# Key products behind each query block, 11 of 16 lists searched before the dense tiles: one change to a fused decoder layer on one core

## Chip, cores and metric

One core of a Trainium2 chip runs the whole layer in one launch. The metric is the device time of the program in microseconds (us); lower is better. Engines are written as in the profile: PE is the matrix engine, DVE the vector engine, ACT the scalar engine, POOL the GpSimd engine, SP the queue that issues most loads.

## What is computed

A decoder layer over 512 tokens of width 1024: a mixer (short convolution and a gated recurrence), cross-attention into 256 memory tokens, and a retrieval layer (PEER). The change lies almost wholly in the retrieval layer:

```
q = (tokens @ w_query).reshape(Ntok, 8, 2, 128)            # 8 heads, 2 halves: 16 queries of 128
s = einsum('nhpd,hpkd->nhpk', q, sub_keys)                  # 16 lists of 128 scores per token
s_top, i_top = top_k(s, 16)                                 # the 16 best of each list
cand = s_top[:, :, 0, :, None] + s_top[:, :, 1, None, :]    # per head: sums of a pair of lists
best, pos = top_k(cand, 16); gate = softmax(best)           # 16 experts per head
y = sum over h, e of gate_e * gelu(expert_down[e] . x) * expert_up[e]
```

There are 16384 experts (128 blocks of 128).

## The kernel before, in words

Tokens stand in four tiles of 128. Tiles 0 to 2 are "dense": for them the kernel multiplies all 16384 down rows with the tokens (128 **down blocks**, each 24 matrix products over 352 token columns), builds a gate matrix with zeros where an expert isn't chosen, and multiplies with all up rows. Tile 3 (`ST`) is "sparse": its 128 chosen rows per token are gathered from memory by POOL (indirect DMAs) and DVE takes the dot products. The last 32 tokens of dense tile 2 (the "edge") are treated in the same way, with 32 further gathers. So there are 160 gathers and 160 dots in all.

Every weight block is loaded by SP into a ring of 5, rounded by ACT (`high`, L577), and the rest is computed by POOL (`low`, L457). PE waits for `low_ready` of a block, ACT's `high(p)` waits until PE is done with block p-3, and `ahead(b)` is `high(b+2)`. In the retrieval layer the order of work is written out by hand on each engine:

- **Query blocks.** PE computes 16 of them (`columns(68 + n, ...)`), the first eight over 512 tokens and the others over 384. They give list 8 to 15 first and then 0 to 7 (for the sparse tile, lists 0 to 7 come from raw weights before). ACT copies each out (L780, L782).
- **Key products.** PE multiplies queries with keys, 128 by 128 each, in float32. For the sparse tile four groups of four (L1707) are done, two ahead of the query blocks, two behind query block 8. For the dense tiles, 12 groups of four (L1733) follow behind the last query block, each copied out by ACT (L802).
- **Choice.** DVE (`top16`) searches lists: `max` (L1177), `max_index` and `match_replace` (L1181, L1182), `max` (L1186), `max_index` (L1190). `choose` then makes candidates (L1204 to L1210), searches those, writes L1217 (`best_ready`), and turns positions into indices (L1221 to L1246). It is done for the sparse tile first, whose end (L1265, `idx_ready`) lets POOL gather. Then come the dense tiles in the order 2, 0, 1 (`CHOSEN`). Tile 2 ends with L1288 (`idx_ready` 2), the others with gate pieces (L1277 to L1280, `hk_ready` 1 and 2). Between the searches DVE does dots (L1170): 12 in the score lists of a tile, 4 in the candidates, 6 in the rest, 66 in all (`DOTS_A`).
- **Down blocks before the gates.** Meanwhile PE does `AHEAD` = 60 down blocks. PE's `first_product(i)` also waits for the `gelu` of block i-2. ACT's `early_at(i)` is `high` for block i+2, then `gelu` of block i (L814), then a store (L816). Behind `EXP_AT` = 16, 32, 52 blocks ACT waits for `best_ready` of a tile and takes an exponential (L840); behind two more blocks of the first group it waits for `idx_ready` 2 and moves edge indices (L848). Ahead of block 40 and of block 59 PE waits for `hk_ready` 1 and 2 and transposes (L1776).
- **Gate steps.** 48 of them follow, each beside a down block (L1748), with about 1.7 gathers and dots each, and then the remaining 20 down blocks with 14 gathers (`DOTS_END`). Then come the up blocks, 128 of 18 products.

POOL's loop at that place is `low(84 + i)`, then gathers `down_row(k)`: 5 at i = 0, 2 at i = 1, and from there about 1.13 per block, in a ring of 7 slots. Gather k waits until the dot of k-7 is done.

Of the kernel before, what the change touches and what calls it, by code (L numbers as in the profile page):

```python
# [13 lines left out]
P = 128  # L14
# [14 lines left out]
NK = 128  # L29
# [13 lines left out]
CHOSEN = (DT - 1,) + tuple(range(DT - 1))  # L43
EXP_AT = (16, 32, 52)
TURN_AT = (20, 40, 60)
AHEAD = TURN_AT[-1]
# [20 lines left out]
ROWS = SLOTS + EDGE_SLOTS  # L67
FIRST_EDGE = 44
GEL_AT, SPLIT_AT, LAST_TURN = 12, 20, 28
DOTS_SCORES = (3, 3, 3, 3)  # L70
DOTS_CAND = (1, 1, 1, 1)
DOTS_HOT = 6
DOTS_A = DT * (sum(DOTS_SCORES) + sum(DOTS_CAND) + DOTS_HOT)
DOTS_STEP = (0, 0) + (2,) * 10 + (1, 2, 2) * 12
DOTS_END = (1,) * 14
ROWS1, COLS2 = 3, 4
CANDS = ROWS1 * TK + (TK - ROWS1) * COLS2
UPPER = 0xFFFF0000
FIRST_GATHER = 0
KEEP = 16  # L80
# [23 lines left out]
def build(nc, x_in, mem_in, vecs_in, final_in, ffn_in, front_w, keys_in, down_in, down_rows, up_in, out, gate_dram, hid_dram):  # L104
    ctx = ExitStack()
    with ctx:
# [104 lines left out]
        dense_k, sparse_k = TopK(108, 124, 5), TopK(184, 92, 2)  # L211
        hk = dense_k.hk
        esum = at(27.75, 16)
        hkT = at(132.5, 5 * DN // 2).bitcast(BF16).rearrange("p (a n r) -> p a n r", a=5, r=2)
# [61 lines left out]
        QB = (6, 7, 0, 1)  # L276
        SB = (0, 1, 2, 0)
        KEY_ORDER = (2, 3, 0, 1)
        PB = (0, 2, 4, 5, 0, 2, 4, 5, 0, 2, 0, 2)
        bank_free = sem("bank_free")  # L280
# [13 lines left out]
        qp_out, pk_done, pk_out = sem("qp_out"), sem("pk_done"), sem("pk_out")  # L294
        KS = 4
        qs_out = sem("qs_out")
# [136 lines left out]
        def _(pool):  # L433
# [57 lines left out]
            for i in range(AHEAD + 2):  # L491
                low(FRONT + i)
                if i == FIRST_GATHER:
                    pool.wait_ge(idx_ready, 1)
                    while k < 5:
                        down_row(k)
                        k += 1
                if i == FIRST_GATHER + 1:
                    while k < RING_A:
                        if k == 5:  # L500
                            pool.wait_ge(pk_done, KS + 4 * DT)
                        down_row(k)
                        k += 1
                while k < DOTS_A and i > FIRST_GATHER and (k - RING_A) * (AHEAD - 8 - FIRST_GATHER) < (i - FIRST_GATHER - 1) * (DOTS_A - RING_A):
                    down_row(k)
                    k += 1
# [30 lines left out]
        def _(act):  # L537
# [49 lines left out]
            def ahead(b):  # L587

                high(b + 2)
# [72 lines left out]

            def keys_out(block, b):
                ahead(block)
                act.wait_ge(block_used, block + 1)
                nc.scalar.activation(KT[:, b, :], psum[:, b % 2, 0:NM], ACT.Copy).then_inc(k_out, 1)
# [13 lines left out]
            nc.scalar.activation(junk[:, SEQ:2 * SEQ], junk[:, 0:SEQ], ACT.Exp, scale=-0.5).then_inc(conv_root, 1)  # L680
            keys_out(31, 3)
            for b in range(32, 36):
                ahead(b)
                act.wait_ge(conv_y, CC + b - 31)
                nc.scalar.activation(hT_half[0][:, b - 32, :], pB[:, b - 32, :], ACT.Copy).then_inc(y_high, 1)
            values_out(0, 2)
            for b in range(4, 8):
                keys_out(32 + b, b)
            def kv_high_part(n):
# [94 lines left out]

            sparse_query_out(0)
            norm_high(ffnn)
            high(QPOS)
            sparse_query_out(1)
            high(QPOS + 1)
            sparse_key_out(0)  # L790
            sparse_key_out(1)
            for n in range(16):
                query_out(n)
                if n == 8:
                    sparse_key_out(2)
                    sparse_key_out(3)
            for c in range(4 * DT):
                if c == 8:
                    high(USED + 2)
                act.wait_ge(pk_done, KS + c + 1)  # L800
                g = KEY_ORDER[c // DT]
                nc.scalar.activation(score[:, c % DT, g * 512:(g + 1) * 512], psum[:, PB[c], :], ACT.Copy)\  # L802
                    .then_inc(pk_out, 1)
                if c == 3:
                    act.wait_ge(best_ready, 1)
                    nc.scalar.activation(sparse_k.ebest, sparse_k.ebest, ACT.Exp).then_inc(e_ready, 1)
            def early_at(i):
# [13 lines left out]

            for i in range(4):
                early_at(i)
# [126 lines left out]
        def _(dve):  # L950
# [243 lines left out]

            def choose(scores, u, k, between_scores, between_cand, between_hot, hk, hk_free, copied=(None,)):

                for part, groups in enumerate(copied):
                    if groups is not None:
                        dve.wait_ge(pk_out, groups)
                    each = 16 // len(copied)  # L1200
                    k = top16([(scores[:, j * NK:(j + 1) * NK], u.top[:, j, :], u.topi[:, j, :].bitcast(U32))
                               for j in range(part * each, (part + 1) * each)], k, between_scores)
                pairs = u.pairs.bitcast(BF16).rearrange("p (a r) -> p a r", r=2)
# [48 lines left out]
            def gates_of(u, dst, exps):  # L1252
# [10 lines left out]
            step(nc.vector.tensor_copy(psum[:, 3, 0:P], at(205.5, P)))  # L1263
            choose(score[:, ST, :], sparse_k, 0, (0, 0, 0, 0), (0, 0, 0, 0), 0, sparse_k.hk, 0, (2, KS))
# [8 lines left out]
            dve.wait_ge(pk_out, KS + 4 * DT)  # L1273
            kd = 0
# [7 lines left out]
            for n, t in enumerate(CHOSEN):  # L1282
                kd = choose(score[:, t, :], dense_k, kd, DOTS_SCORES, DOTS_CAND, DOTS_HOT, hk if n else hk_last, max(n - 1, 0))
                if n:
# [140 lines left out]
        def _(pe):  # L1425
# [289 lines left out]
            pe.wait_ge(ffnn.ready, KC)  # L1715
            pe.wait_ge(ffns.high, 2)
            for n in range(16):
                if n >= 4:
                    pe.wait_ge(qp_out, n - 3)
                columns(68 + n, hT_half, SEQ if n < 16 - RAW else DN, 4 + n % 4)  # L1720
                if n == 8:
                    pe.wait_ge(qp_out, 8)
                    sparse_keys(2)
                    pe.wait_ge(pk_out, 1)
                    sparse_keys(3)
            pe.wait_ge(pk_out, KS)
            for c in range(4 * DT):
                g, t = KEY_ORDER[c // DT], c % DT
                pe.wait_ge(qp_out, max(c // DT * 4 + 4, {4: 13, 5: 14}.get(PB[c], 0)))
                if c >= 4:  # L1730
                    pe.wait_ge(pk_out, KS + (c - 1 if c >= 10 else c - 3))
                for hp in range(4 * g, 4 * g + 4):
                    ins = nc.tensor.matmul(psum[:, PB[c], hp % 4 * NK:(hp % 4 + 1) * NK], qpT[:, hp, t * P:(t + 1) * P],  # L1733
                                           keysT[:, hp, :], start=True, stop=True)
                ins.then_inc(pk_done, 1)

# [30 lines left out]

            pe.wait_ge(pk_out, KS + 8)
            def turn_indices(n, indices, split):
# [8 lines left out]

            for i in range(AHEAD):
                if i == TURN_AT[1]:  # L1780
                    turn_indices(1, hk, hk[:, 2:5, :])
# [78 lines left out]
```

## Time and profile before

| | us |
|---|---|
| median of 3 runs (lowest, highest) | 1619.19 (1617.63, 1620.11) |
| the profiled execution's own time | 1619.37 |
| its span, first to last instruction | 1617.6 |
| PE busy in the span | 1597.2 |
| DVE, ACT, POOL busy | 1140.9, 665.7, 820.0 |

The 1.8 us between the span and the time of the execution lie around the program. A row of the timeline reads: start, duration, engine and line, operation, what it wrote and read, how many such instructions in a row, and in brackets how long the engine had been idle before and who released it.

### The profile page before, as it was taken

The numbers are of one execution on the slowest core, as the hardware profiler recorded it, in microseconds if no ns is written. First come the engines' busy times: TensorE is split into PE (matmuls) and PEld (weight loads), VectorE is DVE, ScalarE is ACT, GpSimd is POOL, SyncE is SP. The second block draws the span as 40 slices with busy tenths as digits, with TensorE's granted clock in tenths as the row PEclk, the third lists the DMA queues.
The fourth block names the chain that finished last, engine by engine and source line by source line (L and its number), as shares of the span: only waits on it lengthen the run. The fifth ranks groups of instructions, "written<-read, shape, count | busy, mean of one in ns | idle before, by whom it ended". The sixth has DMA issues, their size and how long they took to land.

```text
span 1617.6 us, 25384 instructions
## 1 busy us (share of the span) xinstructions
PE 1597.2 (99%) x9227; PEld 1423.1 (88%) x9227; DVE 1140.9 (71%) x2214; ACT 665.7 (41%) x995; POOL 820.0 (51%) x523
## 2 busy tenths in 40 slices
PE   8999999999999999999999999999999999999998
PEld 6888888888889999999999999998888888888886
DVE  4155451351509999997999997339888888888887
ACT  5352442441534344434444544443333333333333
POOL 4463276423244989996877777856222222222220
PEclk9999999999999999999999999999999999999999
DMA  5332243313434999997999999949999999999992
GB/s 196 92 103 71 76 150 96 104 53 118 151 97 136 348 338 337 333 349 236 330 407 400 400 412 402 357 145 398 396 337 348 333 350 334 350 335 347 340 330 77
DMA packets 154442, 424.96 MB, mean 263 GB/s; under 512 B 15728, under 2 KB 65904, under 8 KB 154224
## 3 DMA queue, kind: packets, MB, share of 16 engines
q1 hardware_dynamic: 89088, 229.41, 41.5%
q0 software_dynamic: 41472, 151.01, 25.2%
q10 hardware_dynamic: 23792, 43.33, 7.0%
q8 instruction: 58, 0.95, 0.2%
q14 instruction: 32, 0.26, 0.0%
HBM read 379.88 MB, written 43.25 MB: 262 GB/s over the span
## 4 chain that ended last, share of the span: by engine, by line
PE 90%; DVE 4%; ACT 2%; POOL 2%; DMA 1%; issue 1%; DVEq 0%; SPq 0%; ACTq 0%
PE psum L1459 28%; PE psum L1461 27%; PE psum L1460 27%; PE psum L1748 4%; POOL w_low L457 1%; DMA hid_dram<-arena 1%; PE psum L1695 1%; ACT kept L547 1%; POOL arena L486 1%; DVE arena L1069 0%; ACT w_high L577 0%; PE psum L1582 0%; DMA kept<-x_in 0%; DVE hT_low L1041 0%; PE psum L1431 0%
## 5 line engine op out<-in xcount | busy, mean ns | idle before, releaser
L457 POOL TENSOR_TENSOR w_low<-kept,w_high 128x1024 fp32r<-128x1024 f32 x212 | 520.1, 2457 | 309.3 <-ACT w_high L577 307.5
L1459 PE MATMUL psum<-hT_high,w_high 128*128 128x352 f32 (+2 forms) x1408 | 483.9, 344 | 6.2 <-POOL w_low L457 6.1
L1461 PE MATMUL psum<-hT_high,w_low 128*128 128x352 f32 (+2 forms) x1408 | 477.1, 339 | 0.0
L1460 PE MATMUL psum<-hT_low,w_high 128*128 128x352 f32 (+2 forms) x1408 | 476.5, 338 | 0.0
L1459 PE MATMUL psum<-up_high,wgt_high 128*128 128x512 f32 x768 | 299.0, 389 | 0.0
L1460 PE MATMUL psum<-up_low,wgt_high 128*128 128x512 f32 x768 | 299.0, 389 | 0.0
L1461 PE MATMUL psum<-up_high,wgt_low 128*128 128x512 f32 x768 | 299.0, 389 | 0.0
L1459 PEld LDWEIGHTS psum<-hT_high,w_high 128*128 128x128 f32 x1408 | 265.3, 188 | 21.6 <-ACT arena L814 3.7
L577 ACT ACTIVATE w_high<-kept 128x1024 fp32r<-128x1024 f32 x212 | 223.7, 1056 | 128.1 <-PE psum L1461 91.2
L1460 PEld LDWEIGHTS psum<-hT_low,w_high 128*128 128x128 f32 x1408 | 265.1, 188 | 12.4 <-issue 0.5
L1461 PEld LDWEIGHTS psum<-hT_high,w_low 128*128 128x128 f32 x1408 | 264.8, 188 | 12.6
L581 ACT ACTIVATE up_high<-arena 128x1024 fp32r<-128x1024 f32 x128 | 135.8, 1061 | 314.3 <-PE psum L1461 310.1
L1170 DVE CUSTOM_DVE_ANT_0 arena<-arena,psum 128x1024 f32<-128x1024 f32 x160 | 190.4, 1214 | 37.0 <-DMA arena<-down_rows,kept 36.4
L1341 DVE TENSOR_TENSOR up_low<-arena,up_high 128x1024 fp32r<-128x1024 f32 x128 | 156.8, 1225 | 79.1 <-ACT up_high L581 79.1
L1461 PEld LDWEIGHTS psum<-up_high,wgt_low 128*128 128x128 f32 x768 | 144.2, 188 | 30.0
L1460 PEld LDWEIGHTS psum<-up_low,wgt_high 128*128 128x128 f32 x768 | 144.2, 188 | 29.8
L1459 PEld LDWEIGHTS psum<-up_high,wgt_high 128*128 128x128 f32 x768 | 144.2, 188 | 29.8
L532 POOL DMA_INDIRECT arena<-up_in,kept x64 | 66.8, 1044 | 185.7 <-DVE kept L1349 175.8
L486 POOL DMA_INDIRECT arena<-down_rows,kept x128 | 121.9, 953 | 64.5 <-DVE kept L1170 31.8
L532 POOL DMA_INDIRECT kept<-up_in,kept x64 | 66.0, 1031 | 170.9 <-DVE kept L1349 159.4
L814 ACT ACTIVATE arena<-psum 128x352 f32<-128x352 f32 x112 | 52.0, 464 | 206.0 <-PE psum L1461 179.6
L1313 DVE TENSOR_TENSOR arena<-arena,psum 128x3072 bf16<-128x3072 bf16 x48 | 83.8, 1745 | 0.0
(251 smaller groups left out, 1956.4 us busy)
## 6 DMA issues: line engine op xcount, KB each, us to landing
kept<-down_in SPq DMA_DIRECT2D x128, 512.0 KB, 6.6
arena<-up_in SPq DMA_DIRECT2D x128, 512.0 KB, 5.7
kept<-front_w SPq DMA_DIRECT2D x92, 512.0 KB, 3.6
gate_dram<-arena ACTq DMA_DIRECT2D x40, 512.0 KB, 8.9
hid_dram<-arena ACTq DMA_DIRECT2D x112, 176.0 KB
arena<-hid_dram SPq DMA_DIRECT2D x112, 176.0 KB, 5.1
kept<-gate_dram SPq DMA_DIRECT2D x24, 640.0 KB, 8.3
arena<-gate_dram SPq DMA_DIRECT2D x8, 640.0 KB, 8.8
```

What stands on the lines that cost most here:

```text
L457: nc.gpsimd.tensor_tensor(lower, ring[:, p % RING, :], high.bitcast(F32), ALU.subtract).then_inc(low_ready, 1)
L486: nc.gpsimd.indirect_dma_start(ring[slot], None, down_rows, bass.IndirectOffsetOnAxis((edge_idx if edge else idx3)[:, j:j + 1].bitcast(U32 ...
L532: nc.gpsimd.indirect_dma_start(rows_c[k % RING_C], None, up_rows, bass.IndirectOffsetOnAxis(idx3[:, k:k + 1].bitcast(U32), 0))\
L577: nc.scalar.activation(w_half(p)[0], ring[:, p % RING, :], ACT.Copy).then_inc(high_ready, 1)
L581: nc.scalar.activation(up_hi[:, s % 4, :], uraw[:, up_slot(s), :], ACT.Copy).then_inc(up_high, 1)
L1170: nc.vector.tensor_tensor_reduce(ring[slot], ring[slot], h_row, 1.0, 0.0, ALU.mult, ALU.add, (edge_dot if edge else dot3)[:, j:j + 1]).the ...
L1313: nc.vector.tensor_tensor(hot_g[:, s], hot_i.rearrange("p (n q) i r -> p n q i r", q=1).to_broadcast(each), pieces[:, m:m + PAIRS].rearran ...
L1341: nc.vector.tensor_tensor(up_lo[:, up_slot(s), :], uraw[:, up_slot(s), :], up_hi[:, s % 4, :].bitcast(F32), ALU.subtract).then_inc(up_low, 1)
L1459: nc.tensor.matmul(out, lhs[0], rhs[0], start=first, stop=False)
L1460: nc.tensor.matmul(out, lhs[0], rhs[1], start=False, stop=False)
L1461: return nc.tensor.matmul(out, lhs[1], rhs[0], start=False, stop=last)
L1748: ins = nc.tensor.matmul(psum[:, (2 * n + m) % 3, t % 4 * P:(t % 4 + 1) * P], hot_j[:, n % HOTS, t // 2, :, t % 2], hot_g[:, n % HOTS, t / ...
```

## The change

Constants: `EXP_AT` becomes 14, 26, 41 and `TURN_AT` 18, 34, 48, so `AHEAD` is 48, PE waits for `hk_ready` ahead of blocks 34 and 47, and 32 down blocks follow behind the 48 gate steps. `DOTS_SCORES` goes from 3 to 2 each, so that a dense tile holds 18 dots in place of 22 and `DOTS_A` is 54. `DOTS_END` has 26 gathers in place of 14. The edge gathers begin at the 33rd in place of the 45th.

Key products: `key_products(n)` is one product per tile (4 for n below 8, otherwise 3) for one list, issued by PE behind query block n+1; the last one stands behind down block 0. ACT copies each out in one instruction (`key_out`). Only two sparse groups stay ahead of the query blocks.

DVE: while query blocks run, it searches the sparse list of block n and, for n = 0 to 6, the same list of the three dense tiles. After the sparse `choose` it searches four more lists of each dense tile (n = 7 to 10). Each dense tile then copies these eleven lists into place (four copies) and searches the other five.

POOL: the 6th and 7th gathers move from i = 1 to i = 2, and the eighth and later ones come from i = 6 on, 1.2 per block. ACT: `high` for block 76 stands between the two halves of the norm's copies, and around block 32 `ahead(b + 1)` takes the place of `ahead(b)` ahead of each wait for `conv_y`.

```diff
-EXP_AT = (16, 32, 52)
-TURN_AT = (20, 40, 60)
+EXP_AT = (14, 26, 41)
+TURN_AT = (18, 34, 48)
...
-FIRST_EDGE = 44
+FIRST_EDGE = 32
...
-DOTS_SCORES = (3, 3, 3, 3)
+DOTS_SCORES = (2, 2, 2, 2)
+EARLY, MORE = 8, 3
...
-DOTS_END = (1,) * 14
+DOTS_END = (1,) * 26
...
+FIRST_GATHER, FIRST_DOT = 0, 5
...
-        KS = 4
+        KS = 2
+        KEYS = KS + 16
...
-                if i == FIRST_GATHER + 1:
+                if i == FIRST_GATHER + 2:
...
-                while k < DOTS_A and i > FIRST_GATHER and (k - RING_A) * (AHEAD - 8 - FIRST_GATHER) < (i - FIRST_GATHER - 1) * (DOTS_A - RING_A):
+                while k < DOTS_A and k - RING_A < (i - FIRST_DOT) * 6 // 5:
...
+            ahead(32)
             for b in range(32, 36):
-                ahead(b)
+                ahead(b + 1)
                 act.wait_ge(conv_y, CC + b - 31)
...
+            def key_out(n):
+                j, tiles = (n + RAW) % 16, NT if n < 16 - RAW else DT
+                act.wait_ge(pk_done, KS + n + 1)
+                nc.scalar.activation(score[:, 0:tiles, j * NK:(j + 1) * NK],
+                                     psum[:, DB[n % 2], 0:tiles * NK].rearrange("p (t k) -> p t k", k=NK), ACT.Copy).then_inc(pk_out, 1)
...
-            norm_high(ffnn)
+            norm_high(ffnn, range(4))
             high(QPOS)
+            norm_high(ffnn, range(4, KC))
...
+                if n:
+                    key_out(n - 1)
+                if n == 14:
                     act.wait_ge(best_ready, 1)
...
+            early_at(0)
+            key_out(15)
+            for i in range(1, 4):
...
+            dve.wait_ge(pk_out, KS)
+            top16(lists_of(ST, [place(sparse_k, j) for j in range(RAW)]), 0, none)
+            for n in range(EARLY):
+                dve.wait_ge(pk_out, KS + n + 1)
+                top16(lists_of(ST, [place(sparse_k, RAW + n)]) + (early_lists(n) if n < EARLY - 1 else []), 0, none)
+            choose(sparse_k, 0, none, 0, sparse_k.hk, 0)
...
+            for n in range(EARLY - 1, EARLY + MORE):
+                dve.wait_ge(pk_out, KS + n + 1)
+                top16(early_lists(n), 0, none)
...
+                for to, early, more in ((dense_k.top, early_top[t], more_top[t]),
+                                        (dense_k.topi.bitcast(U32), early_topi[t].bitcast(U32), more_topi[t].bitcast(U32))):
+                    step.put(nc.vector.tensor_copy(to[:, RAW:RAW + EARLY, :], early))
+                    step.put(nc.vector.tensor_copy(to[:, 0:MORE, :], more))
+                kd = top16(lists_of(t, [place(dense_k, j) for j in range(MORE, RAW)]), kd, DOTS_SCORES)
...
+            def key_products(n):
+                j, bank = (n + RAW) % 16, DB[n % 2]
+                pe.wait_ge(qp_out, n + 1)
+                pe.wait_ge(pk_out, KS + n - 1 if n >= 2 else 1)
+                for t in range(NT if n < 16 - RAW else DT):
+                    ins = nc.tensor.matmul(psum[:, bank, t * NK:(t + 1) * NK],
+                                           qpT_s[:, j, :] if t == ST else qpT[:, j, t * P:(t + 1) * P],
+                                           keysT[:, j, :], start=True, stop=True)
+                ins.then_inc(pk_done, 1)
...
+                if n:
+                    key_products(n - 1)
```

## Rows read from the trace of the kernel before

**Rows 1.** Timeline of PE: its waits for POOL, the last key products, first down blocks.
```profile
225.13 0.36 PE L1459 MATMUL psum<-memT_high,w_high 128*128 128x256 f32 x1 [1.43 <-POOL w_low L457]
...
431.32 0.47 PE L1459 MATMUL psum<-hT_high,w_high 128*128 128x512 f32 x1 [0.89 <-POOL w_low L457]
...
519.56 2.02 PE L1733 MATMUL psum<-arena 128*128 128x128 f32 x16 [0.42 <-ACT arena L802]
...
521.34 0.41 PE L1459 MATMUL psum<-hT_high,w_high 128*128 128x352 f32 x1
...
526.55 0.40 PE L1459 MATMUL psum<-hT_high,w_high 128*128 128x352 f32 x1 [1.09 <-POOL w_low L457]
...
531.32 0.40 PE L1459 MATMUL psum<-hT_high,w_high 128*128 128x352 f32 x1 [0.68 <-POOL w_low L457]
```
**Rows 2.** Timeline of ACT: copies behind query blocks, gelu behind down blocks, key copy.
```profile
442.52 0.49 ACT L780 ACTIVATE arena<-psum 128x384 f32<-128x384 f32 x1 [3.83 <-PE psum L1461]
...
447.96 0.49 ACT L780 ACTIVATE arena<-psum 128x384 f32<-128x384 f32 x1 [3.83 <-PE psum L1461]
...
481.12 0.60 ACT L774 ACTIVATE arena<-psum 128x512 f32<-128x512 f32 x1 [0.30 <-PE psum L1707]
...
485.29 0.49 ACT L780 ACTIVATE arena<-psum 128x384 f32<-128x384 f32 x1 [2.61 <-PE psum L1461]
...
489.45 0.49 ACT L780 ACTIVATE arena<-psum 128x384 f32<-128x384 f32 x1 [2.72 <-PE psum L1461]
...
579.52 0.46 ACT L814 ACTIVATE arena<-psum 128x352 f32<-128x352 f32 x1 [1.40 <-PE psum L1461]
...
583.39 0.46 ACT L814 ACTIVATE arena<-psum 128x352 f32<-128x352 f32 x1 [1.87 <-PE psum L1461]
```
**Rows 3.** Timeline of DVE: eight sparse lists, the sparse choice, start of dense tile 2.
```profile
481.82 1.65 DVE L1177 MAX8 arena<-arena 128x8 f32<-128x128 f32 x8 [40.30 <-ACT arena L774]
...
491.70 1.93 DVE L1204 CAST arena<-arena 128x512 bf16<-128x512 uint32 x1
...
517.15 0.29 DVE L1265 SCALAR_TENSOR_TENSOR kept<-arena 128x128 uint32<-128x128 f32 x1
...
522.32 0.87 DVE L1177 MAX8 arena<-arena 128x8 f32<-128x128 f32 x4 [1.59 <-ACT arena L802]
```
**Rows 4.** Timeline of DVE: a dot, then marks of the three dense tiles.
```profile
553.59 1.22 DVE L1170 CUSTOM_DVE_ANT_0 arena<-arena,psum 128x1024 f32<-128x1024 f32 x1
...
554.73 2.81 DVE L1204 CAST arena<-arena 128x512 bf16<-128x512 uint32 x1
...
591.60 2.73 DVE L1288 SCALAR_TENSOR_TENSOR kept<-arena 128x128 uint32<-128x128 f32 x1
...
597.90 3.19 DVE L1177 MAX8 arena<-arena 128x8 f32<-128x128 f32 x16
...
671.60 3.18 DVE L1177 MAX8 arena<-arena 128x8 f32<-128x128 f32 x16
...
705.26 0.43 DVE L1204 CAST arena<-arena 128x512 bf16<-128x512 uint32 x1
...
745.13 0.29 DVE L1280 TENSOR_TENSOR arena<-psum,arena 128x128 f32<-128x128 f32 x1
```
**Rows 5.** Timeline of ACT and PE: who waits for DVE's choice (exponential of tile 0, last transposes).
```profile
651.43 0.31 ACT L840 ACTIVATE arena<-arena 128x128 f32<-128x128 f32 x1 [0.17 <-DVE arena L1217]
...
753.36 0.71 PE L1776 MATMUL psum<-kept,arena 128*128 128x128 f32 x5
```
**Rows 6.** Timeline of POOL: a gather and a subtraction.
```profile
539.63 0.95 POOL L486 DMA_INDIRECT arena<-down_rows,kept  x1 [0.16 <-DVE kept L1170]
...
540.60 2.44 POOL L457 TENSOR_TENSOR w_low<-kept,w_high 128x1024 fp32r<-128x1024 f32 x1
```
**Rows 7.** DMA issues of 520 to 750 us: count, size, median us from issue to landing.
```profile
arena<-down_rows,kept POOLq DMA_INDIRECT x43, 7.1
```
**Rows 8.** Stretches of the end: busy us (count) of PE, PEld, DVE, ACT, POOL; granted clock; DMA.
```profile
1612.00:1617.00 5.00, 0.00 (x0) 0.00 (x0) 2.56 (x3) 1.51 (x5) 0.00 (x0) 0.72 0.54 210
```

More of the change, by code:

```diff
@@ L78 @@
 UPPER = 0xFFFF0000
-FIRST_GATHER = 0
+FIRST_GATHER, FIRST_DOT = 0, 5
 KEEP = 16
@@ L212, in build @@
         hk = dense_k.hk
+        early_top, early_topi = ([at(kb + j, EARLY * TK, EARLY, TK) for kb in (205.5, 206.5, 99)] for j in (0, 0.5))
+        more_top, more_topi = ([at(92 + 0.375 * t + j, MORE * TK, MORE, TK) for t in range(DT)] for j in (0, 0.1875))
         esum = at(27.75, 16)
@@ L276, in build @@
         QB = (6, 7, 0, 1)
-        SB = (0, 1, 2, 0)
-        KEY_ORDER = (2, 3, 0, 1)
-        PB = (0, 2, 4, 5, 0, 2, 4, 5, 0, 2, 0, 2)
+        SB = (0, 1)
+        DB = (2, 0)
         bank_free = sem("bank_free")
@@ L497, in _ @@
                         k += 1
-                if i == FIRST_GATHER + 1:
+                if i == FIRST_GATHER + 2:
                     while k < RING_A:
                         if k == 5:
-                            pool.wait_ge(pk_done, KS + 4 * DT)
+                            pool.wait_ge(pk_done, KEYS)
                         down_row(k)
                         k += 1
-                while k < DOTS_A and i > FIRST_GATHER and (k - RING_A) * (AHEAD - 8 - FIRST_GATHER) < (i - FIRST_GATHER - 1) * (DOTS_A - RING_A):
+                while k < DOTS_A and k - RING_A < (i - FIRST_DOT) * 6 // 5:
                     down_row(k)
@@ L661, in _, with keys_out @@
                     conv_square(2)
-            def keys_out(block, b):
-                ahead(block)
+            def keys_out(block, b, begun=False):
+                if not begun:
+                    ahead(block)
                 act.wait_ge(block_used, block + 1)
@@ L687, in _ @@
             for b in range(4, 8):
-                keys_out(32 + b, b)
+                keys_out(32 + b, b, begun=b == 4)
             def kv_high_part(n):
@@ L793, in _ @@
                 query_out(n)
[L794 to L804, printed above, removed]
+                if n:
+                    key_out(n - 1)
+                if n == 14:
                     act.wait_ge(best_ready, 1)
                     nc.scalar.activation(sparse_k.ebest, sparse_k.ebest, ACT.Exp).then_inc(e_ready, 1)
+            high(USED + 2)
             def early_at(i):
@@ L820, in early_tiles @@
                     early_at(i)
-            for i in range(4):
+            early_at(0)
+            key_out(15)
+            for i in range(1, 4):
                 early_at(i)
@@ L1193, in top16, with lists_of, choose @@
                 return k
[L1195 to L1202, printed above, removed]
+            def lists_of(t, places):
+                return [(score[:, t, j * NK:(j + 1) * NK], top, topi.bitcast(U32)) for j, top, topi in places]
+            def choose(u, k, between_cand, between_hot, hk, hk_free):
                 pairs = u.pairs.bitcast(BF16).rearrange("p (a r) -> p a r", r=2)
@@ L1263, in _, with place, early_lists @@
             step(nc.vector.tensor_copy(psum[:, 3, 0:P], at(205.5, P)))
-            choose(score[:, ST, :], sparse_k, 0, (0, 0, 0, 0), (0, 0, 0, 0), 0, sparse_k.hk, 0, (2, KS))
+            none = (0, 0, 0, 0)
+            def place(u, j):
+                return j, u.top[:, j, :], u.topi[:, j, :]
+            def early_lists(n):
+                j = (n + RAW) % 16
+                return [pair for t in range(DT) for pair in lists_of(
+                    t, [(j, early_top[t][:, n, :], early_topi[t][:, n, :]) if n < EARLY else
+                        (j, more_top[t][:, n - EARLY, :], more_topi[t][:, n - EARLY, :])])]
+            dve.wait_ge(pk_out, KS)
[4 more added lines that the diff above has]
+            choose(sparse_k, 0, none, 0, sparse_k.hk, 0)
             nc.vector.scalar_tensor_tensor(idx3.bitcast(U32), sparse_k.hk[:, 0, :], float(NK), sparse_k.hk[:, 1, :],
@@ L1271, in _ @@
             step(nc.vector.tensor_copy(own_h, h_chunks))
-            dve.wait_ge(pk_out, KS + 4 * DT)
+            dve.wait_ge(pk_out, KEYS)
             kd = 0
@@ L1282, in _ @@
             for n, t in enumerate(CHOSEN):
-                kd = choose(score[:, t, :], dense_k, kd, DOTS_SCORES, DOTS_CAND, DOTS_HOT, hk if n else hk_last, max(n - 1, 0))
+                for to, early, more in ((dense_k.top, early_top[t], more_top[t]),
[3 more added lines that the diff above has]
+                kd = top16(lists_of(t, [place(dense_k, j) for j in range(MORE, RAW)]), kd, DOTS_SCORES)
+                kd = choose(dense_k, kd, DOTS_CAND, DOTS_HOT, hk if n else hk_last, max(n - 1, 0))
                 if n:
@@ L1720, in _ @@
                 columns(68 + n, hT_half, SEQ if n < 16 - RAW else DN, 4 + n % 4)
[L1721 to L1735, printed above, removed]
+                if n:
+                    key_products(n - 1)
             def first_product(i):
@@ L1766, in second_product @@
                 ins.then_inc(up_done, 1)
-            pe.wait_ge(pk_out, KS + 8)
             def turn_indices(n, indices, split):
@@ L1779, in _ @@
             for i in range(AHEAD):
+                if i == 1:
+                    key_products(15)
                 if i == TURN_AT[1]:
+                    pe.wait_ge(pk_out, KEYS)
                     turn_indices(1, hk, hk[:, 2:5, :])
```

## The prediction

> **What bounds the kernel now.** I began with the page's busy times: PE is busy for 1597.2 of 1617.6 us and DVE for 1140.9, so the kernel is PE's stream of products, and a change gains only what it takes out of PE's gaps. The second view is the timeline of PE, read for starts that come later than the rhythm. Around the change there are few: 1.43 us at 225 us, 0.89 ahead of the first query block, 0.42 in the key products, and then the starts of the first down blocks [rows 1]. An undisturbed down block takes 3.87 us (583.39 less 579.52) [rows 2]. The first took 526.55 - 521.34 = 5.2 and the second 531.32 - 526.55 = 4.8; a third row like it follows. All wait for POOL, whose subtraction stands behind five and then two gathers. The third view is the timeline of DVE and of those who wait for it: the exponential of the second dense tile started 0.17 us after DVE released it [rows 5]. DVE has no time to spare there, which matters below. DVE had been idle for 40.3 us while the query blocks ran [rows 3].
>
> **What is taken away.**
> (a) Block 37's `high` moves ahead of a wait for DVE around 220 us. POOL then has it while it finishes the block before, and PE's wait of 1.43 goes [rows 1]. ACT's copies ahead of the output product start at most 1 us later and DVE reads them later still. Take 1.4 (0 to 1.6).
> (b) `high` of block 76 goes into ACT's gap between two transposes. PE's wait of 0.89 goes [rows 1]. If the weight lands late it stays: 0 to 0.9, take 0.9.
> (c) The key products are the same 64, at 1.78/8 = 0.22 each (521.34 - 519.56 for eight), and only the wait of 0.42 goes. In their new places they wait for nothing: the copy that key product n needs was made one block earlier, and a copy of 0.60 fits in a block [rows 1, 2].
> (d) The start of the down blocks. With no gathers at i = 1 and from 3 to 5, POOL has one subtraction of 2.44 per block of 3.87 and even five gathers (some 6.3 us) end before block 1's subtraction is due, since DVE's sparse choice ends earlier (below). The excess of three blocks goes: 1.3 + 0.9 + 0.9 = 3.1 [rows 1, 6]. From i = 6, a gather and a subtraction take 0.95 + 2.44 + 0.16 = 3.55 and a fifth of a further gather 0.25, 3.8 against 3.87: just enough.
> In all 1.4 + 0.9 + 0.4 + 3.1 = 5.8.
>
> **What DVE does, and when.** Count from the start of the first query block (431.32 before). The eight wide query blocks take 5.44 (447.96 - 442.52), the others 4.16 (489.45 - 485.29) [rows 2]. With key products between them (0.89 for four, 0.67 for three), block 8 ends at 8 x 5.44 + 4.16 + 7 x 0.89 = 53.9. The last sparse key product and its copy end at 55.5. A list costs DVE (491.70 - 481.82)/8 = 1.23 [rows 3], so four lists fit in a block, 21 dense lists really are free, and the sparse choice begins at 56.7. It takes 517.44 - 491.70 = 25.7 and ends at 82.4 (before: 86.1, so POOL's gathers start 3.7 earlier). For the gates DVE then waits for ACT's exponential, which now stands behind query block 14 and `key_out(13)`: 43.5 + 29.1 + 10.5 + 1.6 = 84.7. Then come 12 more lists, 14.8, and the small work that filled 517.44 to 522.32 less 1.59 of idle time, 3.3 [rows 3]. So the first dense tile starts at 102.8, where before it was 522.32 - 431.32 = 91.0. Those twelve lists are not free; they were only put first.
> The dense tiles took 745.42 - 522.32 = 223.1. In the score lists of one, 554.73 - 522.32 = 32.4 holds 12 dots of 1.14 (554.73 - 553.59), which leaves 1.17 per list [rows 3, 4]. Eleven lists and four dots fewer are 12.9 + 4.6 = 17.5 per tile, 52.4 in all. The four copies have no row; 0.29 for 128 elements (L1280) gives 1.2 per tile, and one that meets a POOL subtraction costs as the cast did, 2.81 in place of 0.43, so 3.6 at most. I take 1.6, 4.8 in all [rows 4]. DVE ends with the third tile at 102.8 + 223.1 - 52.4 + 4.8 = 278.3, and was at 314.1 before: 36 us earlier.
>
> *The copies and the skill.* The cast at 554.73 ran 2.4 longer than that at 705.26, while POOL subtracted [rows 4]. The Trainium skill (SBUF - State Buffer, "SBUF: two separate sides") says that DVE and GpSimd share a port pair as an exclusive lock, so that the loser waits out the whole instruction. By that rule one wait per group of copies, not one per copy, is the most, which is my 3.6; with POOL busy without a pause it would be paid nearly each time and the end would be 6 us later.
>
> **What PE does in that time.** Down block 0 starts at 76.8 + 53 x 0.2225 = 88.6, key product 15 costs 0.7, and block i ends at 93.1 + 3.87 i. PE asks for the third tile ahead of block 47, at 93.1 + 46 x 3.87 = 271.1. Before, it asked at 753.36, 7.9 after DVE's end at 745.42 [rows 4, 5]. So PE's question moves up by 51 and DVE's answer by 36: a slack of 7.9 turns into a wait of 278.3 - 271.1 = 7.2.
> ACT's waits lead to the same. The second tile starts at 102.8 + 75.6 - 17.5 + 1.6 = 162.5. Its `best_ready` came 53.4 after its start (651.3 - 597.90), now 37.5: 200.0 [rows 4, 5]. Behind ACT's wait are queued the exponential, `high` of block 28, then POOL's subtraction (2.44): 203.9, but PE could start block 28 at 197.6. That is 6.3 of the 7.2. For `idx_ready` 2, which ACT meets behind block 15, the same sum gives 158.9 + 4.2 = 163.1 against block 18 at 158.9, 4.2 of the 7.2. They don't add up, since each delay moves PE's later questions, and the largest counts.
> One thing adds to it. Gathers are tied to down blocks by POOL's queue and land 7.1 us after the issue [rows 7]. A tile now wants eight dots within 16 us, more than the 1.2 per 3.87 that come. When ACT's first stall holds `high` back, POOL's subtractions and with them gathers 22 to 26 move back by some 4 to 7 us, and the dots of the second tile's score lists wait. By this count gather 23 lands at 178 and is wanted at 174.5. I put 3 on it (0 to 7).
> Behind the turn nothing is left to gain or lose: gate steps, 106 dots and the last gather at down block 121 are as before, and PE had no gap there.
>
> **Sum.** On the profiled execution's own 1619.4 (0.2 above the median, span plus 1.8): 1619.4 - 5.8 + 7.2 + 3.0 = 1623.8.
>
> **Rivals.**
> *R1, DVE in time, faster.* The three tiles lost different amounts to POOL (of two casts of one form one took 2.4 longer [rows 4]). With some 2.4 less in each of the first parts and the copies at 1.2, DVE would end 5 to 7 earlier, and the wait falls to 0 to 2: 1619.4 - 5.8 + 1 = 1614.6. For it: such waits of DVE for POOL came and went between tiles that do the same work. Against it: the 12 lists ahead of the dense tiles have to be paid, and three separate waits all come out late. It decides if DVE starts its first dense tile before 97 on my count.
> *R2, the wait stays but gathers are not late:* 1619.4 - 5.8 + 4 to 8 = 1617.6 to 1621.6, about even.
> *R3, PE's clock.* The page shows a granted clock of nine tenths or more in each of its 40 slices, and 0.72 stands in the last 5 us, where PE did nothing [rows 8]. The change makes waits of 4 to 8 us. If the clock drops to 1.2 GHz behind one, one down block takes 3.9 longer; were it behind the last wait, the time would be 1627.7. The Trainium skill (TensorE: Matmul & The Clock Gate, "HAM oscillation") says that idle gaps make PE return at the lower clock, which speaks against a change that opens such gaps. That stretch agrees in direction [rows 8]; none of before shows work at the lower level.
> *R4, POOL the bound.* With 3.8 of 3.87 used and 1.2 gathers per block, DMA traffic rises by 3%; if POOL needs 3.95, PE loses 3 us over 40 blocks, but DVE's wait would cover it. It adds nothing unless R1 holds.
>
> **How the numbers follow.** Within 0.2% (3.2 us) a measurement of this kernel can't tell a change. The forecast (wait of 7 to 13, 1621 to 1627) has 0.50, R1 0.18, R2 0.20, R3 with longer delays 0.12. Of the forecast a fifth lies below 1622.4. So faster (below 1616.0) 0.18, same 0.29, slower 0.53. The range goes from R1's edge to R3's middle, 1615 to 1629; the forecast's own is 1620.5 to 1628.
>
> **What would show it.** In the changed profile: no idle time ahead of blocks 1 to 3 and ahead of the first query block; the first dense MAX8 about 102.8 behind the first query block; L1204 of the sparse tile at 56.7; ACT idle some 5 to 10 us ahead of the exponential of the second and third dense tile, with DVE as releaser; PE idle for 4 to 8 us in two or three places between down blocks 18 and 47; DVE idle on DMA in front of dots. Wrong would be a DVE that is ready when ACT asks, or a PE without gaps above 1 us. Then the time is 1613 to 1616.

## The result and the profile after

A little slower: 1631.62 us (1624.88 to 1635.19, 6 runs) against 1619.65 before (6 runs), a ratio of 1.0069 with a 95% interval of 1.0053 to 1.0085. The sign was forecast, but the time lies above the range's end of 1629. The profiled execution took 1624.88 (span 1623.1), the least of the six. A second set, in e1, gave 1628.64 and a profiled execution of 1632.05.

The timeline of PE answers to [rows 1]. Around 230 us, and from the down blocks on:

```profile
228.41 0.39 PE L1489 MATMUL psum<-memT_high,w_high 128*128 128x256 f32 x1 [1.89 <-ACT arena L670]
...
593.65 0.63 PE L1489 MATMUL psum<-hT_high,w_high 128*128 128x352 f32 x1 [3.45 <-POOL w_low L460]
594.09 0.49 PE L1490 MATMUL psum<-hT_low,w_high 128*128 128x352 f32 x1
594.38 0.49 PE L1491 MATMUL psum<-hT_high,w_low 128*128 128x352 f32 x1
...
599.57 0.32 PE L1491 MATMUL psum<-hT_high,w_low 128*128 128x352 f32 x1
599.73 0.32 PE L1489 MATMUL psum<-hT_high,w_high 128*128 128x352 f32 x1
...
710.99 0.76 PE L1803 MATMUL psum<-kept,arena 128*128 128x128 f32 x5 [2.15 <-DVE arena L1305]
```

The waits among the first down blocks are gone. In their place PE waits 3.45 us ahead of block 18 (the name in the bracket is POOL's, which itself came late) and 2.15 for DVE ahead of block 47. Behind each wait, directly or 1 us later, the products start 0.29 apart (594.38 less 594.09), and later 0.16 again (599.73 less 599.57); 28 of them are slow, 18 behind the first wait and 10 behind the second. The windows show why. In each row the granted clock is the third number from the end, behind the busy times (and counts) of PE, PEld, DVE, ACT and POOL:

```profile
586.00:590.00 4.00, 4.00 (x27) 3.92 (x25) 3.85 (x7) 0.00 (x0) 0.00 (x0) 1.00 0.95 374
590.00:594.00 4.00, 0.55 (x3) 0.38 (x2) 3.93 (x14) 2.82 (x4) 2.71 (x2) 0.83 0.73 229
594.00:598.00 4.00, 4.00 (x15) 4.00 (x15) 4.00 (x24) 1.06 (x1) 3.83 (x3) 0.50 0.57 182
598.00:602.00 4.00, 4.00 (x23) 4.00 (x22) 2.50 (x9) 1.12 (x2) 3.51 (x4) 0.82 0.68 160
602.00:606.00 4.00, 4.00 (x27) 4.00 (x27) 0.94 (x2) 1.68 (x3) 3.82 (x3) 1.00 0.93 320
```

From 594 to 598 PE did 15 products where an undisturbed stretch holds 27, at a clock of 0.50, the 1.2 GHz level. What held block 18 up is in the timelines of ACT, then POOL, then DVE:

```profile
590.01 1.06 ACT L580 ACTIVATE w_high<-kept 128x1024 fp32r<-128x1024 f32 x1 [6.99 <-DVE kept L1318]
```
```profile
584.64 0.95 POOL L489 DMA_INDIRECT arena<-down_rows,kept  x1 [0.16 <-issue]
591.15 2.36 POOL L460 TENSOR_TENSOR w_low<-kept,w_high 128x1024 fp32r<-128x1024 f32 x1 [5.56 <-ACT w_high L580]
593.65 0.95 POOL L489 DMA_INDIRECT arena<-down_rows,kept  x1
```
```profile
535.88 1.33 DVE L1310 COPY arena<-arena 128x128 f32<-128x128 f32 x1
...
598.94 1.22 DVE L1178 CUSTOM_DVE_ANT_0 arena<-arena,psum 128x1024 f32<-128x1024 f32 x1 [0.93 <-DMA arena<-down_rows,kept]
601.71 1.22 DVE L1178 CUSTOM_DVE_ANT_0 arena<-arena,psum 128x1024 f32<-128x1024 f32 x1 [0.56 <-DMA arena<-down_rows,kept]
607.17 1.22 DVE L1178 CUSTOM_DVE_ANT_0 arena<-arena,psum 128x1024 f32<-128x1024 f32 x1 [4.23 <-DMA arena<-down_rows,kept]
611.51 1.22 DVE L1178 CUSTOM_DVE_ANT_0 arena<-arena,psum 128x1024 f32<-128x1024 f32 x1 [0.66 <-DMA arena<-down_rows,kept]
...
710.65 0.29 DVE L1305 TENSOR_TENSOR arena<-psum,arena 128x128 f32<-128x128 f32 x1
```

The rows show a loop. ACT stood idle for 6.99 us until DVE had made its choice of the first dense tile; POOL, queued behind ACT's rounding, issued no gather between 584.64 and 593.65; and DVE's dots of the second tile then waited for gathers, 6.9 us in all with one more wait of 0.54. The first dense tile began at 535.88, 104.7 behind the first query block (431.21), and the third ended at 279.7.

Behind that PE has no wait of note in either kernel. From the last transposes ahead of the gate steps to the end of the span it needs 1617.6 - 753.4 = 864.2 us before and 1623.1 - 711.0 = 912.1 here, and 12 more down blocks of 3.87 and the slow products account for the difference.

### The profile page after: what moved, and what is told of

Its sections match the earlier page's. It is cut to its first block, busy times and chain, and to the rows that moved or that the text cites. A ratio compares the mean times of both kernels' runs of the same rounds, so it can differ in the third digit from the quotient of the medians.

```text
span 1623.1 us, 25417 instructions
## 1 busy us (share of the span) xinstructions
PE 1601.0 (99%) x9227; PEld 1426.4 (88%) x9227; DVE 1139.0 (70%) x2226; ACT 666.8 (41%) x997; POOL 819.9 (51%) x523
## 4 chain that ended last, share of the span: by engine, by line
PE 55%; DVE 3%; DMA 1%; POOL 1%; ACT 0%; issue 0%; DVEq 0%
PE psum L1489 17%; PE psum L1490 17%; PE psum L1491 17%; PE psum L1776 4%; DVE arena L1178 1%; DMA arena<-down_rows,arena 1%; POOL w_low L460 0%; DVE arena L1251 0%; POOL arena L489 0%; DVE arena L1215 0%; DVE psum L1262 0%; DVE arena L1185 0%; DVE arena L1240 0%; ACT kept L950 0%; DVE arena L1310 0%
```

## Experiments

Ratios are to the kernel before, run on the same chip.

**e1. The changed kernel again.**

> The changed kernel once more, unaltered, timed and profiled. If DVE's lateness with the clock behind it is the cause, the time differs between executions because each short wait of PE may or may not be followed by a stretch at the lower clock: 1624 to 1636, and a second profile shows PE waits of 2 to 8 us at down blocks 18, 28, 43 or 47, each with 3 to 6 us of slow products behind it. If the cause were steady work (more products, slower blocks), the times would lie within 3 us of each other.

1628.64 us (5 runs, 1626.10 to 1632.05), ratio 1.0058 (1.0045 to 1.0072), so times differ by more than the 3 us of the rival. Its profiled execution took 1632.05, 7.2 more than the first. PE's list of waits, 515 to 1625 us, has one row (total, times, longest):

```profile
PE psum L1489 <- POOL w_low L460: 11.0, 3, 3.8
```

So there are three waits of 3.72, 3.78 and 3.55 (11.0 against 5.6 in the first profile), and 31 products start 0.29 apart, 10 or 11 behind each wait. That is 1.3 to 1.4 us behind each, not the 3 to 6 expected. DVE waited 8.1 us for gathers in the second tile and ended the third 286.5 behind the first query block, 7 later than in the first profile.

**e2. All questions later.** A question is a place where ACT or PE waits for a result of DVE: `EXP_AT` sets ACT's, `TURN_AT` PE's.

```
-EXP_AT = (14, 26, 41)
-TURN_AT = (18, 34, 48)
-DOTS_END = (1,) * 26
+EXP_AT = (16, 29, 44)
+TURN_AT = (20, 36, 52)
+DOTS_END = (1, 1, 1, 1, 2) * 4 + (1, 1)
```

> The changed kernel with ACT's and PE's questions to DVE put 2 to 4 blocks later: EXP_AT 16, 29, 44, TURN_AT 20, 36, 52, and the 26 last gathers in 22 blocks. DVE-late theory: no wait of PE above 1 us between down blocks 4 and 52, granted clock 1.00 there, 1615 to 1617. Rival (1.2 gathers per block or the key products between the query blocks cost PE its rhythm): still above 1622.

1618.13 us (11 runs), ratio 1.0003 (0.9990 to 1.0016). One wait of PE is left, 0.59 us, no product is slow, and the gather waits of DVE in the second tile fall to 1.9 us. The rival is out. The time is 10.5 us below e1's on the same chip (13.5 below the first set's), so the questions' places carry the loss; the plan of the gathers before the gates is the same as in the changed kernel. The median is still 1.1 above the expected range; the profiled execution, at 1614.80, was the fastest of the eleven.

**e3 and e4. Two edits alone on the kernel before**, one run each.

```
+            ahead(32)
             for b in range(32, 36):
-                ahead(b)
+                ahead(b + 1)
...
-                keys_out(32 + b, b)
+                keys_out(32 + b, b, begun=b == 4)
```
```
-            norm_high(ffnn)
+            norm_high(ffnn, range(4))
             high(QPOS)
+            norm_high(ffnn, range(4, KC))
```

> The kernel before with only ACT's order around block 32 changed. Theory from the changed profile: POOL no longer pauses, DVE's third and fourth two-input product each wait for a whole subtraction, the last ACT copy comes at about 226.5 in place of 222.4, and PE waits 1.9 us for a key copy in place of 1.4 for POOL: about 1 us slower than before at the first output product (235.5 in place of 234.5). Rival (as forecast): the wait of 1.4 goes, 233.0.

> The kernel before with only high of block 76 moved between the two halves of the norm's copies. Both theories: PE starts the first query block at about 430.3 in place of 431.3 and keeps the 1.0 us. If the weight lands late it stays at 431.3.

e3: the first output product, at 234.46 before, comes at 235.45, as expected. The wait of 1.43 for POOL [rows 1] is replaced by one of 1.88 for ACT. This edit costs 1.0 us where I booked a gain of 1.4. The totals (1623.93 and 1618.39) are single runs and decide nothing. In the changed kernel the timelines of POOL and DVE show the cause, and e3's own have the same rows within 0.1 us:

```profile
209.40 16.50 POOL L460 TENSOR_TENSOR w_low<-kept,w_high 128x1024 fp32r<-128x1024 f32 x6 [1.43 <-ACT w_high L580]
```
```profile
220.74 2.90 DVE L1082 TENSOR_TENSOR hT_low<-arena,hT_high 128x512 fp32r<-128x512 f32 x1
223.56 2.88 DVE L1077 SCALAR_TENSOR_TENSOR arena<-arena,kept 128x512 f32<-128x512 f32 x1
226.37 0.68 DVE L1082 TENSOR_TENSOR hT_low<-arena,hT_high 128x512 fp32r<-128x512 f32 x1
```

POOL now has six subtractions without a pause (four before, then 2.24 us idle). DVE's operations with two operands in SBUF take 2.9 while POOL subtracts (16.50/6 = 2.75 each) and 0.68 once it stops; before, POOL's pause let three of them pass at 0.7. ACT's copies, and PE behind them, wait for DVE. The Trainium skill (SBUF — State Buffer, "SBUF: two separate sides") gives the rule that the loser of the shared port pair waits for the winner's whole instruction; the trace agrees, and I had applied it to the copies but not here.

e4: the first query block starts at 430.14 in place of 431.32 and down block 0 at 520.15 in place of 521.34. The wait of 0.89 and a little more, 1.2 in all, is gained.

**e5. Work in the waits.**

```
+                if i in (18, 28, 43, 47):
+                    pe.wait_ge(gelu_out, i + 1)
+                    for _ in range(22):
+                        nc.tensor.matmul(psum[:, 4 + i % 2, 0:DE], hT_half[0][:, 0, 0:P], hT_half[0][:, 0, 0:DE],
+                                         start=True, stop=True)
```

> The changed kernel with 22 additional 352-column products ahead of the products of down blocks 18, 28, 43 and 47, into the block's own PSUM bank, whose first real product starts the sum afresh, so they change no value. They fill TensorE's waits with work. Theory: what the changed kernel lost is the waits (2 to 4 us each) and, behind each, a stretch in which TensorE's clock was granted at its lower level and some 20 to 31 products came at 0.29 us in place of 0.16 (about 2 us each). With the waits filled the granted clock should stay at 1.00 around 590 to 715, the products behind the waits come at 0.16 from the start, and the time falls by the last such stretch at least (1.6 us, if VectorE's end at 711 sets the time) and by all three at most (6 us): 1622 to 1627. Rival: the lower clock doesn't hang on the waits; then the stretches stay, and the time is 1629 to 1633.

1634.74 us (4 runs), outside what both said, and badly designed: I left out that 88 more products cost 88 x 0.16 = 14.1 us wherever there is no wait to fill. At block 18 the wait for the `gelu` remained, 2.59 us, and the clock still fell behind it (0.77 from 589 to 595). At the three other places there was no wait, and the granted clock is 1.00 in every stretch from 600 us on. This fits a clock that falls behind waits and doesn't prove it; the time tells nothing.

**e6. Gathers one block sooner**: `FIRST_DOT` 4 in place of 5.

> The changed kernel with the eighth and later gathers from the fifth down block on, one block (3.9 us) sooner. Theory: VectorE's dot products of the second and third tile wait 7 to 8 and 2 to 4 us for gathers, because each is issued too few microseconds ahead of its use; one block sooner should take those sums to about 3 and 1, VectorE ends 5 to 7 us sooner, and the last question is answered within its time: 1623 to 1627. Rival: the waits are those of the transfers' rate in this stretch and not of their start; then the sums stay within 1.5 us of the changed kernel's and the time is 1628 to 1632. A second rival: more GpSimd work among the first down blocks brings back waits of TensorE for GpSimd there, some 3 us.

1624.83 us (4 runs), ratio 1.0040 (1.0024 to 1.0055): 3.8 us less than e1 on the same chip, within the forecast. One big wait is left, 4.04 at block 18, with 11 slow products; DVE's third tile ends at 278.4 behind the query's start, and no wait stands at the last question. The gather waits fell less than I expected, from 6.9 (first profile) and 8.1 (e1) to 5.4 in the second tile where I said 3, and they are 3.1 in the third where I said 1.

**e7. Only the first question later**: `EXP_AT` 16, 26, 41 and `TURN_AT` 20, 34, 48.

> The changed kernel with the first question put after down block 26 and its turn before 28 in place of 16 and 18 (exponentials at 16, 26, 41, turns at 20, 34, 48); the last question stays. Theory: VectorE's end sets the end of the stage, so a wait at the first question only takes from the later ones: TensorE's wait moves from block 18 to the later question, and the time stays within 2 us of the changed kernel's, 1627 to 1632. Rival: the waits and the stretches at the lower clock add up, and without the first (3.5 us of wait and 2.6 us of slower products) the time is some 6 us less, 1622 to 1624.

1626.42 us (4 runs, 1623.25 to 1631.86), a little outside both ranges and between them: 2.2 us less than e1 on the same chip, 5.2 less than the first set. Without the stop at block 18 DVE's gather waits in the second tile are 1.9 us, with the same gather plan. PE's waits now are 1.12, 0.92 and, behind the third tile's exponential, 4.02. That put the prediction's "the largest counts" in doubt and called for a cleaner set.

**e8 and e9. Questions late enough, ACT's old order at conv block 32.** e9 is the base of what follows:

```
-EXP_AT = (14, 26, 41)
-TURN_AT = (18, 34, 48)
+EXP_AT = (16, 30, 45)
+TURN_AT = (20, 37, 52)
...
-            ahead(32)
             for b in range(32, 36):
-                ahead(b + 1)
+                ahead(b)
...
-                keys_out(32 + b, b, begun=b == 4)
+                keys_out(32 + b, b)
```

(e8: 16, 30, 46 and 20, 37, 54. `DOTS_END` is e2's in e9 and `(1, 1, 2) * 6 + (1, 1)` in e8.)

> The changed kernel with its questions still later than in e2 (exponentials at 16, 30, 46, turns at 20, 37, 54, the last piece behind the last block) and ScalarE's order around conv block 32 as in the kernel before. Theory: no wait of TensorE for VectorE is left, so the time is the kernel before less 1.2 (norm order), less about 3.5 (waits for GpSimd and for key products in the first down blocks): 1614 to 1616, with less scatter than e2, whose second question had under 1 us to spare. Rival: the end of the stage holds something else that waits for the last piece, ScalarE's copies and exponentials at the end, and the time is that of the kernel before, 1618 to 1620.

> The questions of e8 with the last one 2 blocks less late (exponentials at 16, 30, 45, turns at 20, 37, 52, end pieces as in e2) and ScalarE's order around conv block 32 as before. In e8's trace VectorE was idle for 14.9 us behind its last piece, and TensorE waited 2.9 us for ScalarE further on (760 to 1100), where the kernel before and the changed kernel don't wait. Theory: the last question was put off too far, and its work pushed what comes behind it; with it at block 52 that wait goes: 1613 to 1615.5, below e8's 1616.5. Rival: the 2.9 us hang on something else of that stretch, and the time stays at 1616 to 1617.

e8: 1616.51 us (11 runs), ratio 0.9979 (0.9970 to 0.9988). e9: 1617.11 (10 runs), ratio 0.9981 (0.9972 to 0.9990). Both beat both kernels by a little, and are equal within their scatter. e8 lies 0.5 above its expected range, and e9's expectation was wrong: PE's wait for ACT further on is still there (2.2 us at 820, in e8 2.9 in two waits), as e9's list of waits shows:

```profile
PE psum L1775 <- ACT arena L893: 2.2, 1, 2.2
PE psum L1488 <- POOL w_low L460: 1.8, 2, 1.1
```

What ACT waits for there I did not follow up.

**e10, e11 and e12. Early questions one by one.** e9 with the first question early (`EXP_AT` 14, `TURN_AT` 18), with the last early (41, 48, one dot a block at the end), and with both.

> e9 with the first question alone as early as in the changed kernel (exponentials behind block 14, turn at 18). VectorE is in time for the others. Theory: one wait of TensorE at block 18 of about 3.5 us, and behind it a stretch of products at 0.29 us in place of 0.16 that costs some 2.6 us; nothing takes them back, so e9 plus 5.5 to 6.5 us, about 1620. Rival: the slow products only fill time that TensorE would have waited anyway, and the cost is the wait alone: e9 plus 3 to 4.

> e9 with the last question alone as early as in the changed kernel (exponentials behind block 41, turn at 48, one dot a block at the end). Theory: VectorE's end at about 279 us after the query's start sets the end of this stage whatever comes ahead of it, so TensorE's waits at the end sum to about 6 us and one or two stretches at the lower clock cost 2 to 3 more: e9 plus 8 to 10, within 3 us of the changed kernel with its old conv order. Rival: the changed kernel's loss is the sum of its three waits; then this one, with one of them, loses 4 to 5 us to e9.

> e9 with both the first and the last question as early as in the changed kernel (exponentials at 14, 30, 41, turns at 18, 37, 48). Alone the first cost 5.6 us over e9's 1617.1 (e10) and the last 5.5 (e11). Theory, formed after e7: the losses add up, since TensorE's stop at the first question also holds up the subtractions and gathers behind it and so VectorE itself (in e10 its dots waited 5.9 us for gathers, in e9 1.2): 1617.1 + 5.6 + 5.5 = 1628.2, within 1.5. Rival, the prediction's own step: each delay moves the later questions, and the largest counts: 1622.5 to 1624.

| | us (runs) | over e9 | PE's waits of 3 us and more | all its waits | slow products |
|---|---|---|---|---|---|
| e9 | 1617.11 (10) | | none | 4.0 | 0 |
| e10, first | 1622.68 (12) | 5.6 | 7.35 | 8.2 | 10 |
| e11, last | 1622.64 (11) | 5.5 | 5.64 | 6.5 | 11 |
| e12, both | 1628.93 (6) | 11.8 | 3.45, 5.58 | 10.8 | 24 |

The losses add up: 5.6 + 5.5 = 11.1 against 11.8 measured. (e12 ran on another chip; by the ratios to the kernel before, 0.9981, 1.0014, 1.0017 and 1.0051, the three losses are 5.3, 5.8 and 11.3.) The rival's 1622.5 to 1624 is far off, and so is my expectation for e11 (8 to 10), which took DVE's end for a floor under the stage; e11's rival (4 to 5) came closer. e10's sum was right, but not its terms: the wait is 7.35 and not 3.5, the slow products cost 1.3 and not 2.6, and 3.1 us of e9's smaller waits are no longer there. PE in e10, e11 and e12, at the questions:

```profile
595.92 0.63 PE L1488 MATMUL psum<-hT_high,w_high 128*128 128x352 f32 x1 [7.35 <-POOL w_low L460]
```
```profile
692.12 0.63 PE L1488 MATMUL psum<-hT_high,w_high 128*128 128x352 f32 x1 [5.64 <-POOL w_low L460]
```
```profile
592.37 0.48 PE L1488 MATMUL psum<-hT_high,w_high 128*128 128x352 f32 x1 [3.45 <-POOL w_low L460]
...
697.81 0.63 PE L1488 MATMUL psum<-hT_high,w_high 128*128 128x352 f32 x1 [5.58 <-POOL w_low L460]
```

The timelines show what the first stop does to DVE. POOL at that place in e9:

```profile
584.08 0.95 POOL L489 DMA_INDIRECT arena<-down_rows,kept  x1 [0.16 <-issue]
...
587.62 0.95 POOL L489 DMA_INDIRECT arena<-down_rows,kept  x1 [0.16 <-issue]
...
591.65 1.01 POOL L489 DMA_INDIRECT arena<-down_rows,kept  x1
```

and in e10, where a gather is followed by none for 12.5 us:

```profile
583.37 0.95 POOL L489 DMA_INDIRECT arena<-down_rows,kept  x1 [0.16 <-issue]
593.41 2.36 POOL L460 TENSOR_TENSOR w_low<-kept,w_high 128x1024 fp32r<-128x1024 f32 x1 [9.10 <-ACT w_high L580]
595.92 0.95 POOL L489 DMA_INDIRECT arena<-down_rows,kept  x1
```

DVE's waits for gathers in the second tile sum to 1.2 in e9, 5.9 in e10, 2.5 in e11 and 7.2 in e12; e9 against e10, with one gather plan, differ in the first question alone.

Why the last wait doesn't shrink when the first is there is to be seen in e11 and e12. In both DVE ends its first tile 157.8 behind the first query block. In e12 the first stop costs PE 3.45 and 12 slow products of 0.13, 5.0 in all. DVE writes the third tile's `best_ready` (L1221), for which ACT waits, at 687.95 in e11 and at 693.66 in e12, counted from the first query block 5.5 later. Question and answer moved together, and the last wait is 5.64 and 5.58:

```profile
687.95 0.30 DVE L1221 TENSOR_TENSOR arena<-arena 128x128 f32<-128x128 f32 x1
```
```profile
693.66 0.29 DVE L1221 TENSOR_TENSOR arena<-arena 128x128 f32<-128x128 f32 x1
```

It doesn't always happen. In the changed kernel's first profile and in e7 the first tile ends at 157.8 as well, and the third tile's `best_ready` comes at 257.7 and 257.9: the stop at block 18 did not move the last answer, and the last wait was 2.15 in place of e7's 4.02, as the prediction's step has it. In e1 it came at 266.6.

## Why the time was missed

- **The sum again, by PE's rows,** for e1's profiled execution, which is the nearer to the first set's median: forecast 1619.4 - 5.8 + 10.2 = 1623.8. Measured: the gains -5.8 + 2.4 for (a) = -3.4, waits 11.0, slow products 4.0, so 1619.4 - 3.4 + 15.0 = 1631.0 against 1632.05. Such a list tells where PE's time went, not what each item caused: PE is held until DVE's answer, so slow products ahead of a later question shorten the wait there. Only those behind the last wait, 1.4 us, surely come on top.
- **The failed step is "They don't add up, since each delay moves PE's later questions, and the largest counts", together with the 3.0 put on the gathers.** The delay moves PE's later questions, but through ACT and POOL it can move DVE's answers as well, since the gathers stand behind the held subtractions. Two early questions put into e9 alone and together cost 5.6, 5.5 and 11.8, and the last answer comes 5.5 later with the first stop than without (e12, e11). The feedback was in the prediction, sized at 3 (0 to 7). On its own count PE asks at 271.1, and DVE's end was to be 278.3, with the feedback 281.3: 10.2 late. In e1 the end is 286.5, 15.4 late, which is 5.2 more. Over all profiles, DVE's gather waits in the second tile are 5.4 to 8.1 us where PE stopped at block 18 (both of the changed kernel, e5, e6, e10, e12) and 1.2 to 2.5 where it didn't (e2, e7, e8, e9, e11). So they are mostly a result of the stop, not of the gather plan.
- **(a), ACT's order at conv block 32, failed:** booked at a gain of 1.4, it costs 1.0 (e3), which is 2.4 of the miss. "POOL then has it while it finishes the block before" is true, but POOL's unbroken train delays DVE's two-operand operations, and "DVE reads them later still" overlooked that ACT's next copies wait for those.
- **The clock stood as a rival instead of a term.** R3 gave one fall of 3.9 us a chance of 0.12. Behind every wait of 2.15 us and more at the early questions comes a stretch at the lower level: 28 slow products in the changed kernel, each 0.29 - 0.16 = 0.13 longer, are 3.6 us, 31 in e1 are 4.0. Each stretch is shorter than R3's whole block (10 to 18 of 24 products), but there are two or three. The Trainium skill (TensorE: Matmul & The Clock Gate, "HAM oscillation") warned that idle gaps bring it; these stretches agree, and the last section has a gap that brought none. With 5.2 for DVE's end, 2.4 for (a) and up to 1.4 for the clock behind the last wait, 1623.8 becomes 1631.4 to 1632.8, against e1's 1632.05.
- **In the changed kernel itself the adding up is less well shown.** Without its first early question (e7) it gains 2.2 us against e1 and 5.2 against the first set, where full addition asks for some 6; and in the first profile the last answer was not moved.
- **The first profiled execution lies near the forecast by luck too.** Its waits are 5.6 and its slow products 3.6: 1625.2 against 1624.88. DVE's last answer was not moved by the stop and its waits came out some 5 us smaller than forecast, which hid (a) and the clock; the working was not right.
- **(b), (c), (d) held.** The first query block starts at 431.21 in spite of the 1.0; e4 alone gains 1.2. No wait of key products or of down blocks 1 to 3 is left.
- **DVE's schedule held in one profile of two.** The first dense tile starts at 104.7 in both (forecast 102.8); the third ends at 279.7 in the first (278.3) and at 286.5 in e1. The four copies cost 1.6, 0.5 and 2.5 us in the first, about as booked.
- **Rivals.** R1 and R2 are out: DVE starts its first dense tile at 104.7 and not before 97, PE waits in both executions profiled, and gathers are late. R4 did not show: besides the wait at block 18, e6, with gathers sooner, has waits for POOL of under 1 us each (e9 has 0.68 and 1.12).

What stays open: why executions of the changed kernel scatter by 10 us. The two profiled ones differ by 7 us in when DVE writes the second tile's `best_ready` (627.93 and 635.00). Of that 1.0 is a later first query block, 1.2 are gather waits, and 4.8 are two kinds of operation beside POOL, the casts of L1209 (1.5 against 3.5 in all) and the additions of L1215 (2.2 against 4.9). The first tile, too, ended at 157.8 in e12 and at 161.7 in e10, and PE's wait at block 18 is longer by just that, 7.35 in place of 3.45. No run tried to hold either fixed.

## What to carry to other kernels

When a question is asked earlier than its answer is ready, price the whole loop: the engine that waits also holds the transfers that the late engine needs, and the waits of several questions can then add up instead of covering each other. Give a wait of PE of several us its price at the lower clock behind it, here 1.3 to 2.3 us (10 to 18 products, 0.13 each), as a term of the sum. Before work is moved off a pause of POOL, look at which two-operand operations of DVE pass in that pause.

## What the runs showed that was not expected

- The 2.15 us ahead of block 47 in the changed kernel were followed by work at the 1.2 GHz level, a granted clock of 0.64 in the next window, while e9's wait of 2.21 at 820, between two groups of 12 gate products in bfloat16 (L1775), was followed by none (1.00). e8's wait at such a place, 1.92 at 870, was followed by 6 slow products (0.57 from 870 to 874). So a shorter wait brought the lower clock where a longer one did not: the length of a wait alone doesn't tell, and what does, no run here separates.

```profile
711.00:715.00 4.00, 4.00 (x19) 4.00 (x20) 2.41 (x4) 1.71 (x3) 1.42 (x1) 0.64 0.33 127
```

- In an unbroken train of POOL's subtractions, consecutive two-operand operations of DVE each last about as long as one subtraction (2.75), 2.9 in place of 0.7 us.
- A shift of three questions by 2 to 4 blocks of 3.87 us, with no work added or removed, moved the time by 10.5 to 13.5 us (e2).
